# Products between matmul streams in the ffn stage and the last stage of a two-block transformer step on one core

## Chip, core and metric

One Trainium2 chip, one of its cores. The metric is the device time of one execution in microseconds.

## What is computed

Two transformer blocks over 256 tokens of 1024 features, fp32. Cut to what matters here:

```python
def conv_ffn(h, w_up, conv_w, conv_b, w_down, rows, cols):
    z = (h @ w_up).reshape(b, rows, cols, 2 * D_FF)
    z = lax.conv_general_dilated(z, conv_w[:, :, None, :], ...)
    z = z.reshape(b, l, 2 * D_FF) + conv_b
    return (jax.nn.silu(z[..., :D_FF]) * z[..., D_FF:]) @ w_down
...
        x = x + mx[:, :, 5] * conv_ffn(h2, ffn_up[layer], ...)   # first block
...
        h2 = rms_norm(x, norm2_g[l])                             # second block
        f = jnp.square(jax.nn.relu(jnp.einsum('bsd,df->bsf', h2, w_mlp1[l])))
        x = x + jnp.einsum('bsf,fd->bsd', f, w_mlp2[l])
```

The first block's ffn has 2 x 2816 inner features (22 chunks of `ffn_up`, 11 of `ffn_down`), the second block's has 4096 (16 chunks of `w_mlp1`, 16 of `w_mlp2`).

## The kernel before

**Tiles.** Activations lie with features on the partitions, as 8 tiles of 128 x 256 tokens. Weights come in chunks of 128 x 2048 through four `raw` buffers (DMA from the sync engine, line 413). ScalarE rounds a chunk to its high part `whi` (line 491), GpSimd (lines 467, 473) or VectorE (line 872) computes the low part `wlo = raw - whi`; there are three buffers of each. VectorE has the low parts of every `w_mlp2` chunk and of `w_mlp1` from chunk 3 on. Activations are split in the same way (H2h and H2l, H4h and H4l, AH and AL, FH and FL).

**Products.** `mm3` (lines 1456 to 1458) is three matmuls of 256 moving columns into one bank of PSUM: high by high, high by low, low by high. `pair` (line 1575) runs one chunk of `ffn_up` or `w_mlp1`: 8 tiles k, two outputs j, three matmuls, 48 in all; its `midway` callback is run ahead of tile n = 5. `contract` (line 1762) runs one chunk of `ffn_down` or `w_mlp2`, again 48 matmuls. Both name the chunk's weights through `weights`, which waits for the high and the low part.

**Small products.** In fp32, so each is two passes on the engine: the profile counts x2.
- `square_columns` (line 1723): a squared tile is the stationary side, a column of ones the moving side, one output column. It sums squares for a norm.
- `rows` (line 1460): a column of RC broadcast to 128 x 128 is stationary, the identity moves (128 columns). It spreads a scale over the partitions.
- `settle` (line 1756): eight products of 128 moving columns. Nobody reads their output.

**Order.** Each engine has one hand-written program, kept together by semaphores. In the ffn stage (line 1784) TensorE runs `ffn_up` 0, settle into banks 6 and 7, `ffn_up` 1 to 4 and then `ffn_up` and `ffn_down` in turn. In the last stage (line 1931) it runs `w_mlp1` 0, with `finish_norm` ahead of its tile 5 (eight column products that end the sum of squares of the last norm), then the two row products, settle into bank 3, `w_mlp1` 1, `w_mlp1` 2, `w_mlp2` 0, `w_mlp1` 3, `w_mlp2` 1 and so on.

**The scale of the last norm.** Columns (`col_x`), ScalarE's root (line 509), VectorE's reciprocal (line 884, `rstd_x`), the row products (`row_x`), ScalarE's copy to RR (line 851, `rr_done`), and VectorE's relu of `w_mlp1` 0, which multiplies by RR (line 1413). VectorE's program in this stage, per i: low parts up to the chunk two places ahead (`low`, line 1407), relu (1413), square (1419), low part of the activation (1423), and from i = 2 the low parts up to two places behind `w_mlp2` i - 2 (line 1426). ScalarE's runs alongside: high parts of weights and, behind each square, FH (line 861):

```python
        for i in range(18):
            if i < 16:
                low(turn["w_mlp1", i] + 2)
                if i == 0:
                    e.wait_ge(s["rr_done"], 3)
...
            if i >= 2:
                low(turn["w_mlp2", i - 2] + 2)
```

Of the kernel before, what the change touches and what calls it, by code (L numbers as in the profile page):

```python
# [14 lines left out]
P = 128  # L15
T = 256
D = 1024
KT = D // P
NH = 4
# [155 lines left out]
def build(nc, io):  # L175
# [6 lines left out]
    start = 16512  # L182
# [1251 lines left out]
    def tensor(e):  # L1434
# [137 lines left out]
                    m = e.matmul(b[:, hd * P:(hd + 1) * P], KM[:, hd, t * P:(t + 1) * P], q, start=True, stop=True)  # L1572
                m.then_inc(s["lev"], 1)

        def pair(name, i, xh, xl, ks=range(KT), ready=None, apart=False, midway=None):
            h, l = weights(name, i)
            bs = [group(name, i), group(name, i, 1)] if apart else [group(name, i)] * 2
            todo = [(n, k, j) for j in range(2) for n, k in enumerate(ks)] if apart else [
                (n, k, j) for n, k in enumerate(ks) for j in range(2)]
            for n, k, j in todo:  # L1580
                if midway and (n, j) == (5, 0):
                    midway()
                if ready and j == 0:
                    ready(k)
                m = mm3(bs[j][:, j * T:(j + 1) * T], h, l, (j * KT + k) * P, xh[:, k, :], xl[:, k, :],
                        n == 0 and (j == 0 or apart), n == len(ks) - 1)
                if n == len(ks) - 1 and (j or apart):
                    m.then_inc(s["gemm"], 1)
# [134 lines left out]
        def square_columns(b, sq, f, n):  # L1723
            for k in range(f, f + n):
                for t in range(2):
                    m = e.matmul(b[:, t:t + 1], sq[:, k, t * P:(t + 1) * P], ones[:, 0:1], start=k + t == 0,  # L1726
                                 stop=k == KT - 1, skip_group_check=True)
            return m
# [24 lines left out]
            e.wait_ge(s["h2_hi"], k + 1)  # L1753
            e.wait_ge(s["h2_lo"], k + 1)

        def settle(banks, w, x):
            for t, b in enumerate(banks):
                for k in range(NH):
                    e.matmul(b[:, k * P:(k + 1) * P], w[:, k, t * P:(t + 1) * P], x[:, k, t * P:(t + 1) * P],
                             start=True, stop=True)  # L1760

        def contract(name, j, xh, xl, slots, hi_sem, lo_sem, per, last):
            h, l = weights(name, j)
            ends_ = last == 2 * j + 1
# [18 lines left out]
            e.wait_ge(s[free[0]], free[1])  # L1783
        for i in range(24):
            if i == 1:
                settle((bank[6], bank[7]), TMP1, SQ1)
            if i < 22:
                pair("ffn_up", i, H2h, H2l, ready=h2_ready if i == 0 else None)
            if i >= 5 and i % 2:
                contract("ffn_down", (i - 5) // 2, AH, AL, NA, "a_hi", "a_lo", 1, 21)  # L1790
# [131 lines left out]

        def finish_norm():
            e.wait_ge(s["sq3_sum"], 2)
            square_columns(bs, SQ3, 0, 2)
            for j in range(2):
                e.wait_ge(s["sq3"], 4 + j)
                m = square_columns(bs, SQ3, 6 + j, 1)
            m.then_inc(s["col_x"], 1)

        for i in range(18):
            if i < 16:
                pair("w_mlp1", i, H4h, H4l, ready=h4_ready if i == 0 else None,
                     midway=finish_norm if i == 0 else None)
                if i == 0:
                    b = misc("rows3")
                    e.wait_ge(s["rstd_x"], 2)
                    rows(b, [wide(0), wide(1)], "row_x")
                    settle((bank[3], bank[3]), SQ3[:, 0:4, :], SQ3[:, 4:8, :])
            if i == 2:  # L1940
                for free in acc2_free:
                    e.wait_ge(s[free[0]], free[1])
            if i >= 2:
                contract("w_mlp2", i - 2, FH, FL, NF, "f_hi", "f_lo", 2, 31)
# [125 lines left out]
```

## Time and profile before

| | |
|---|---|
| median of 3 runs | 725.08 us (724.97, 725.08, 731.91) |
| profiled execution | 724.98 us |
| its span, first to last instruction | 723.0 us |
| mean granted clock of TensorE | 0.995 |
| TensorE busy | 710.7 us (98%) |
| VectorE, ScalarE, GpSimd busy | 483.5, 358.3, 389.1 us |
| HBM read, written | 143.88 MB, 1.05 MB |

PE is TensorE, DVE VectorE, ACT ScalarE, POOL GpSimd, SP the sync engine. The profile shows one execution. A matmul's own duration includes its way through the pipeline, so matmuls overlap: what TensorE gives to each is the distance of the starts, and a chunk's time is the distance between its first start and the next one's. L12 is line 12 of the kernel. Where a line of the timeline has a releaser in brackets, the engine was idle before it for that long.

### The profile page before, as it was taken

The numbers are of one execution on the slowest core, as the hardware profiler recorded it, in microseconds if no ns is written. First come the engines' busy times: TensorE is split into PE (matmuls) and PEld (weight loads), VectorE is DVE, ScalarE is ACT, GpSimd is POOL, SyncE is SP. The second block draws the span as 40 slices with busy tenths as digits, with TensorE's granted clock in tenths as the row PEclk, the third lists the DMA queues.
The fourth block names the chain that finished last, engine by engine and source line by source line (L and its number), as shares of the span: only waits on it lengthen the run. The fifth ranks groups of instructions, "written<-read, shape, count | busy, mean of one in ns | idle before, by whom it ended". The sixth has DMA issues, their size and how long they took to land.

```text
span 723.0 us, 14266 instructions
## 1 busy us (share of the span) xinstructions
PE 710.7 (98%) x5892; PEld 688.6 (95%) x5892; DVE 483.5 (67%) x906; ACT 358.3 (50%) x459; POOL 389.1 (54%) x219
## 2 busy tenths in 40 slices
PE   6899999999999999999999999999999999999998
PEld 3798889999999999999999999999999999999998
DVE  3886898469616459977777774657465666566563
ACT  6679235245434565455555456445754334334331
POOL 0767553547557948897888888765895000000000
PEclk9999999999999999999999999999999999999999
DMA  8995878336634637565655554433445564565611
GB/s 358 420 414 181 349 286 317 154 117 234 233 117 133 217 118 276 179 224 188 217 179 179 202 204 175 141 134 135 164 137 209 192 207 172 205 202 172 210 59 59
DMA packets 21234, 145.84 MB, mean 202 GB/s; under 512 B 2482, under 2 KB 3250, under 8 KB 3891
## 3 DMA queue, kind: packets, MB, share of 16 engines
q1 hardware_dynamic: 21024, 144.87, 55.0%
q8 instruction: 47, 0.77, 0.4%
q14 instruction: 17, 0.13, 0.0%
q10 hardware_dynamic: 146, 0.07, 0.0%
HBM read 143.88 MB, written 1.05 MB: 200 GB/s over the span
## 4 chain that ended last, share of the span: by engine, by line
PE 97%; DVE 1%; ACT 1%; issue 0%; DMA 0%; ACTq 0%; DVEq 0%
PE bank L1456 25%; PE bank L1458 25%; PE bank L1457 25%; PE bank L1475 5%; PE CP L1458 2%; PE CP L1456 2%; PE CP L1457 2%; PE bank L1572 2%; PE bank L1500 1%; PE bank L1533 1%; PE bank L1515 1%; PE CP L1489 1%; PE bank L1482 0%; PE bank L1684 0%; PE bank L1611 0%; PE bank L1726 0%
## 5 line engine op out<-in xcount | busy, mean ns | idle before, releaser
L473 POOL TENSOR_TENSOR wlo<-raw,whi 128x512 fp32r<-128x512 f32 (+1 forms) x185 | 353.3, 1941 | 136.8 <-ACT whi L491 136.7
L491 ACT ACTIVATE whi<-raw 128x2048 fp32r<-128x2048 f32 x100 | 191.3, 1913 | 46.2 <-DMA raw<-in_w_in 25.8
L1213 DVE SCALAR_TENSOR_TENSOR Y<-bank,vec,Y 128x189 f32<-128x189 f32 (+2 forms) x352 | 123.0, 423 | 35.2 <-ACT Y L746 35.2
L1456 PE MATMUL bank<-H2h,whi 128*128 128x256 f32 x352 | 97.7, 278 | 0.0
L1457 PE MATMUL bank<-H2l,whi 128*128 128x256 f32 x352 | 97.2, 276 | 0.0
L1458 PE MATMUL bank<-H2h,wlo 128*128 128x256 f32 x352 | 97.2, 276 | 0.0
L1456 PE MATMUL bank<-H1h,whi 128*128 128x256 f32 (+1 forms) x288 | 89.8, 312 | 2.3 <-ACT H1h L557 2.0
L1458 PE MATMUL bank<-H1h,wlo 128*128 128x256 f32 (+1 forms) x288 | 88.2, 306 | 0.0
L872 DVE TENSOR_TENSOR wlo<-raw,whi 128x2048 fp32r<-128x2048 f32 x29 | 66.7, 2300 | 32.2 <-ACT whi L491 32.2
L1457 PE MATMUL bank<-H1l,whi 128*128 128x256 f32 (+1 forms) x288 | 88.2, 306 | 0.0
L1456 PE MATMUL bank<-H4h,whi 128*128 128x256 f32 x256 | 70.9, 277 | 0.0
L1457 PE MATMUL bank<-H4l,whi 128*128 128x256 f32 x256 | 70.7, 276 | 0.0
L1458 PE MATMUL bank<-H4h,wlo 128*128 128x256 f32 x256 | 70.7, 276 | 0.0
L1456 PEld LDWEIGHTS bank<-H2h,whi 128*128 128x128 f32 x352 | 66.2, 188 | 0.1
L1457 PEld LDWEIGHTS bank<-H2l,whi 128*128 128x128 f32 x352 | 66.2, 188 | 0.1
L1458 PEld LDWEIGHTS bank<-H2h,wlo 128*128 128x128 f32 x352 | 66.2, 188 | 0.0
L1456 PEld LDWEIGHTS bank<-H1h,whi 128*128 128x128 f32 x288 | 54.9, 191 | 6.4 <-issue 3.3
L1458 PEld LDWEIGHTS bank<-H1h,wlo 128*128 128x128 f32 x288 | 54.9, 191 | 2.9
L1457 PEld LDWEIGHTS bank<-H1l,whi 128*128 128x128 f32 x288 | 54.9, 191 | 2.9
L467 POOL TENSOR_TENSOR wlo<-raw,whi 128x512 fp32r<-128x512 f32 x28 | 35.3, 1288 | 27.8 <-ACT whi L494 27.8
L1458 PEld LDWEIGHTS bank<-H4h,wlo 128*128 128x128 f32 x256 | 48.1, 188 | 0.0
L1456 PEld LDWEIGHTS bank<-H4h,whi 128*128 128x128 f32 x256 | 48.1, 188 | 0.0
(337 smaller groups left out, 1920.9 us busy)
## 6 DMA issues: line engine op xcount, KB each, us to landing
raw<-in_w_mlp SPq DMA_DIRECT2D x32, 1024.0 KB, 4.9
raw<-in_w_in SPq DMA_DIRECT2D x30, 1024.0 KB, 5.2
raw<-in_ffn_up SPq DMA_DIRECT2D x22, 1024.0 KB, 4.9
raw<-in_ada_hi SPq DMA_DIRECT2D x16, 1024.0 KB, 5.4
raw<-in_ffn_down SPq DMA_DIRECT2D x11, 1024.0 KB, 4.9
raw<-in_w_out SPq DMA_DIRECT2D x8, 1024.0 KB, 4.9
ada_s<-in_ada_s SPq DMA_DIRECT2D x4, 1024.0 KB, 18.0
ada_p<-in_ada_p SPq DMA_DIRECT2D x2, 1024.0 KB, 10.2
```

The source lines that it names most:

```text
L467: e.tensor_tensor(part(l, kp, 1), part(r, kp, 1), part(h, kp, 1).bitcast(F32), ALU.subtract).then_inc(s["lo_pool"], 1)
L473: m = e.tensor_tensor(l[:, a:a + step], r[:, a:a + step], h[:, a:a + step].bitcast(F32), ALU.subtract)
L491: e.activation(whi[q % NHI][:, :], raw[n % NRAW][:, :], ACT.Copy).then_inc(s["w_hi"], 1)
L872: e.tensor_tensor(l[:, :], r[:, :], h[:, :].bitcast(F32), ALU.subtract).then_inc(s["lo_dve"], 1)
L1213: e.scalar_tensor_tensor(o[:, r0:r1, c0:c1], z[:, r0 + dr:r1 + dr, c0 + dc:c1 + dc], cw[:, f, tap:tap + 1], o[:, r0:r1, c0:c1], ALU.mult, ...
L1456: e.matmul(out, h[:, col:col + P], xh, start=first, stop=False, skip_group_check=True)
L1457: e.matmul(out, h[:, col:col + P], xl, start=False, stop=False, skip_group_check=True)
L1458: return e.matmul(out, l[:, col:col + P], xh, start=False, stop=last, skip_group_check=True)
L1475: m = e.matmul(out, x, w, start=k + t + n == 0, stop=(k, n) == (KT - 1, 2), skip_group_check=True)
L1489: e.matmul(CP[:, half], ones[0:1, 0:P], CROW[:, half], start=True, stop=True).then_inc(s["c_spread"], 1)
L1500: m = e.matmul(out, C2[:, k, :], r[:, :, k, :], start=k == 0, stop=k == KT - 1)
L1572: m = e.matmul(b[:, hd * P:(hd + 1) * P], KM[:, hd, t * P:(t + 1) * P], q, start=True, stop=True)
```

## The change

TensorE's program alone is edited. In the ffn stage, settle between chunks 0 and 1 becomes eight column products of SQ1 into bank 6, and one row product into bank 7 is put between chunks 1 and 2. In the last stage settle is gone, the columns of the norm stand ahead of tile 7 of chunk 0 instead of tile 5 (with all squares waited for at their head), and the row products stand ahead of tile 5 of chunk 1 instead of behind chunk 0. `settle` itself is removed. The outputs of the new products in the ffn stage are read by nobody.

```diff
--- before.py
+++ after.py
@@ -1572,13 +1572,13 @@
                     m = e.matmul(b[:, hd * P:(hd + 1) * P], KM[:, hd, t * P:(t + 1) * P], q, start=True, stop=True)
                 m.then_inc(s["lev"], 1)
 
-        def pair(name, i, xh, xl, ks=range(KT), ready=None, apart=False, midway=None):
+        def pair(name, i, xh, xl, ks=range(KT), ready=None, apart=False, midway=None, at=5):
             h, l = weights(name, i)
             bs = [group(name, i), group(name, i, 1)] if apart else [group(name, i)] * 2
             todo = [(n, k, j) for j in range(2) for n, k in enumerate(ks)] if apart else [
                 (n, k, j) for n, k in enumerate(ks) for j in range(2)]
             for n, k, j in todo:
-                if midway and (n, j) == (5, 0):
+                if midway and (n, j) == (at, 0):
                     midway()
                 if ready and j == 0:
                     ready(k)
@@ -1753,12 +1753,6 @@
             e.wait_ge(s["h2_hi"], k + 1)
             e.wait_ge(s["h2_lo"], k + 1)
 
-        def settle(banks, w, x):
-            for t, b in enumerate(banks):
-                for k in range(NH):
-                    e.matmul(b[:, k * P:(k + 1) * P], w[:, k, t * P:(t + 1) * P], x[:, k, t * P:(t + 1) * P],
-                             start=True, stop=True)
-
         def contract(name, j, xh, xl, slots, hi_sem, lo_sem, per, last):
             h, l = weights(name, j)
             ends_ = last == 2 * j + 1
@@ -1783,7 +1777,9 @@
             e.wait_ge(s[free[0]], free[1])
         for i in range(24):
             if i == 1:
-                settle((bank[6], bank[7]), TMP1, SQ1)
+                square_columns(bank[6], SQ1, 0, NH)
+            if i == 2:
+                rows(bank[7], [wide(0)], None)
             if i < 22:
                 pair("ffn_up", i, H2h, H2l, ready=h2_ready if i == 0 else None)
             if i >= 5 and i % 2:
@@ -1922,21 +1918,19 @@
 
         def finish_norm():
             e.wait_ge(s["sq3_sum"], 2)
+            e.wait_ge(s["sq3"], 5)
             square_columns(bs, SQ3, 0, 2)
-            for j in range(2):
-                e.wait_ge(s["sq3"], 4 + j)
-                m = square_columns(bs, SQ3, 6 + j, 1)
-            m.then_inc(s["col_x"], 1)
+            square_columns(bs, SQ3, 6, 2).then_inc(s["col_x"], 1)
+
+        def finish_rows():
+            b = misc("rows3")
+            e.wait_ge(s["rstd_x"], 2)
+            rows(b, [wide(0), wide(1)], "row_x")
 
         for i in range(18):
             if i < 16:
                 pair("w_mlp1", i, H4h, H4l, ready=h4_ready if i == 0 else None,
-                     midway=finish_norm if i == 0 else None)
-                if i == 0:
-                    b = misc("rows3")
-                    e.wait_ge(s["rstd_x"], 2)
-                    rows(b, [wide(0), wide(1)], "row_x")
-                    settle((bank[3], bank[3]), SQ3[:, 0:4, :], SQ3[:, 4:8, :])
+                     midway={0: finish_norm, 1: finish_rows}.get(i), at=5 if i else 7)
             if i == 2:
                 for free in acc2_free:
                     e.wait_ge(s[free[0]], free[1])
```

TensorE, end of `ffn_up` chunk 0 and start of chunk 1 (bank<-H2h,whi_54 is chunk 0, whi_55 chunk 1; the number behind a buffer tells its copies apart). Before:

```order
L1456 MATMUL bank<-H2h,whi_54 128x256
L1457 MATMUL bank<-H2l,whi_54 128x256
L1458 MATMUL bank<-H2h,wlo_57 128x256
L1759 MATMUL bank<-SQ_130,TMP_131 128x128 x8
L1456 MATMUL bank<-H2h,whi_55 128x256
L1457 MATMUL bank<-H2l,whi_55 128x256
L1458 MATMUL bank<-H2h,wlo_58 128x256
```

After:

```order
L1456 MATMUL bank<-H2h,whi_54 128x256
L1457 MATMUL bank<-H2l,whi_54 128x256
L1458 MATMUL bank<-H2h,wlo_57 128x256
L1726 MATMUL bank<-ones,SQ_130 128x1 x8
L1456 MATMUL bank<-H2h,whi_55 128x256
L1457 MATMUL bank<-H2l,whi_55 128x256
L1458 MATMUL bank<-H2h,wlo_58 128x256
```

Eight products of 128 moving columns have given way to eight of one column. In the new order there is one more, at the end of chunk 1, ahead of chunk 2 (whi_53):

```order
L1456 MATMUL bank<-H2h,whi_55 128x256
L1457 MATMUL bank<-H2l,whi_55 128x256
L1458 MATMUL bank<-H2h,wlo_58 128x256
L1462 MATMUL bank<-con,RC 128x128
L1456 MATMUL bank<-H2h,whi_53 128x256
L1457 MATMUL bank<-H2l,whi_53 128x256
L1458 MATMUL bank<-H2h,wlo_56 128x256
```

This single row product has no counterpart before.

TensorE, last stage, end of chunk 0 (whi_53) and start of chunk 1 (whi_54) before:

```order
L1456 MATMUL bank<-H4h,whi_53 128x256
L1457 MATMUL bank<-H4l,whi_53 128x256
L1458 MATMUL bank<-H4h,wlo_56 128x256
L1462 MATMUL bank<-con,RC 128x128 x2
L1759 MATMUL CP<-SQ_160 128x128 x8
L1456 MATMUL bank<-H4h,whi_54 128x256
L1457 MATMUL bank<-H4l,whi_54 128x256
L1458 MATMUL bank<-H4h,wlo_57 128x256
```

And in the new order, the last six matmuls of chunk 0 with the columns ahead of them, and the first of chunk 1:

```order
L1458 MATMUL bank<-H4h,wlo_56 128x256
L1726 MATMUL bank<-ones,SQ_160 128x1 x8
L1456 MATMUL bank<-H4h,whi_53 128x256
L1457 MATMUL bank<-H4l,whi_53 128x256
L1458 MATMUL bank<-H4h,wlo_56 128x256
L1456 MATMUL bank<-H4h,whi_53 128x256
L1457 MATMUL bank<-H4l,whi_53 128x256
L1458 MATMUL bank<-H4h,wlo_56 128x256
L1456 MATMUL bank<-H4h,whi_54 128x256
```

Settle is gone and the columns have moved from 18 matmuls ahead of the chunk's end to 6. The row products now stand inside chunk 1, behind its 30th matmul:

```order
L1457 MATMUL bank<-H4l,whi_54 128x256
L1458 MATMUL bank<-H4h,wlo_57 128x256
L1462 MATMUL bank<-con,RC 128x128 x2
L1456 MATMUL bank<-H4h,whi_54 128x256
L1457 MATMUL bank<-H4l,whi_54 128x256
L1458 MATMUL bank<-H4h,wlo_57 128x256
```

So they come 30 matmuls later than before, counted from the end of chunk 0.

## Rows read from the trace of the kernel before

**Rows 1.** The page's chain that ended last, by engine (shares of the span).
```profile
PE 97%; DVE 1%; ACT 1%; issue 0%; DMA 0%; ACTq 0%; DVEq 0%
```

**Rows 2.** Timeline of PE, ffn stage: start us, us, engine line operation out<-in xcount.
```profile
267.30 1.95 PE L1759 MATMUL bank<-SQ,TMP 128*128 128x128 f32 x16
...
269.00 0.37 PE L1456 MATMUL bank<-H2h,whi 128*128 128x256 f32 x1
...
274.54 0.28 PE L1456 MATMUL bank<-H2h,whi 128*128 128x256 f32 x1
```

**Rows 3.** Timeline of PE, last stage.
```profile
541.34 0.28 PE L1456 MATMUL bank<-H4h,whi 128*128 128x256 f32 x1
...
544.75 1.86 PE L1726 MATMUL bank<-ones,SQ 128*128 128x1 f32 x16
...
546.47 0.36 PE L1456 MATMUL bank<-H4h,whi 128*128 128x256 f32 x1
...
548.67 0.65 PE L1462 MATMUL bank<-con,RC 128*128 128x128 f32 x4
...
549.16 1.95 PE L1759 MATMUL CP<-SQ 128*128 128x128 f32 x16
...
550.86 0.37 PE L1456 MATMUL bank<-H4h,whi 128*128 128x256 f32 x1
...
556.40 0.28 PE L1456 MATMUL bank<-H4h,whi 128*128 128x256 f32 x1
...
572.72 0.28 PE L1456 MATMUL CP<-FH,whi 128*128 128x256 f32 x1
```

**Rows 4.** Timeline of PE, around a chunk of w_in_2.
```profile
465.00 0.36 PE L1456 MATMUL bank<-H3h,whi 128*128 128x256 f32 x1
...
470.74 0.95 PE L1823 MATMUL bank<-con,SQq 128*128 128x2 f32 x8
```

**Rows 5.** PE by line, 465.3 to 470.7: xcount | busy us, mean ns | idle.
```profile
L1458 PE MATMUL bank<-H3h,wlo 128*128 128x256 f32 x16 | 4.5, 281 | 0.0
```

**Rows 6.** Windows of PE: busy us (x instructions), granted clock, DMA share, GB/s.
```profile
258.50:262.00 3.50, 3.50 (x11) 0.52 0.82 272
...
446.00:453.00 7.00, 7.00 (x64) 1.00 0.41 150
```

**Rows 7.** PE by line, 38 to 50 us.
```profile
L1458 PE MATMUL bank<-H1h,wlo 128*128 128x256 f32 x34 | 9.6, 281 | 0.0
```

**Rows 8.** Timeline of PE, row products in the w_in stage.
```profile
52.72 0.61 PE L1462 MATMUL bank<-con,RC 128*128 128x128 f32 x4
...
53.08 0.37 PE L1456 MATMUL bank<-H1h,whi 128*128 128x256 f32 x1
```

**Rows 9.** PE by line, 53.5 to 58.5 us.
```profile
L1458 PE MATMUL bank<-H1h,wlo 128*128 128x256 f32 x15 | 4.1, 276 | 0.0
```

**Rows 10.** Timeline of DVE, last stage.
```profile
543.70 1.46 DVE L1399 SCALAR_TENSOR_TENSOR H4l<-XR,vec,H4h 128x256 fp32r<-128x256 f32 x1 [0.89 <-ACT H4h L845]
...
549.77 0.69 DVE L1413 SCALAR_TENSOR_TENSOR FR<-bank,RR 128x512 f32<-128x512 f32 x1 [1.28 <-ACT RR L851]
...
553.79 2.51 DVE L872 TENSOR_TENSOR wlo<-raw,whi 128x2048 fp32r<-128x2048 f32 x1 [0.81 <-ACT whi L491]
...
556.60 0.69 DVE L1413 SCALAR_TENSOR_TENSOR FR<-bank,RR 128x512 f32<-128x512 f32 x1 [0.30 <-PE bank L1458]
...
566.66 2.29 DVE L872 TENSOR_TENSOR wlo<-raw,whi 128x2048 fp32r<-128x2048 f32 x1 [1.12 <-ACT whi L491]
...
572.92 0.69 DVE L1413 SCALAR_TENSOR_TENSOR FR<-bank,RR 128x512 f32<-128x512 f32 x1 [1.19 <-PE bank L1458]
```

**Rows 11.** Timeline of POOL, last stage.
```profile
548.23 5.92 POOL L473 TENSOR_TENSOR wlo<-raw,whi 128x512 fp32r<-128x512 f32 x4 [1.94 <-ACT whi L491]
```

**Rows 12.** Timeline of PE, a wait in the middle of a stream.
```profile
31.94 0.36 PE L1456 MATMUL bank<-H1h,whi 128*128 128x256 f32 x1 [1.96 <-ACT H1h L557]
```

**Rows 13.** PE by line, 31.2 to 33 us.
```profile
L1457 PE MATMUL bank<-H1l,whi 128*128 128x256 f32 x3 | 0.8, 279 | 0.0
```

## The prediction

> **What bounds the kernel now.** I read the page's chain of work first. It shows TensorE on 97% of the span, and nearly all of that in the three lines 1456 to 1458, the three products (high by high, high by low, low by high) of `mm3` [rows 1]. Two stages hang on it here: the ffn stage (chunks of `ffn_up` and `ffn_down`, from 261 us) and the last stage (`w_mlp1` and `w_mlp2`, 541 to 720 us). So whatever TensorE is given or spared counts in full, as long as the weights and activations that it reads are ready. The profiled execution took 724.98 us for a span of 723.0 us; the other 1.98 us lies around the span and the change does not touch it. My sum is made against 724.98, 0.10 below the median of 725.08.
>
> Next the timeline of TensorE at both places. In the ffn stage the eight "settle" products (16 passes, since an fp32 product is issued as two) start at 267.30 and the next chunk at 269.00: 1.70 us [rows 2]. That chunk of 48 matmuls takes 5.54 us (269.00 to 274.54). In the last stage chunk 0 starts at 541.34, its 16 column passes at 544.75, its last 18 matmuls at 546.47, the row products at 548.67, settle at 549.16, chunk 1 at 550.86, chunk 2 at 556.40, and the second `w_mlp2` chunk at 572.72 [rows 3]. From 556.40 to 572.72 there are three chunks of 48 matmuls, 5.44 us each, with no gap.
>
> **Two paces.** The extra products have no reader, so I looked for what they might do to their neighbours. The same 48 matmuls take 5.74 us after a burst of column products (465.00 to 470.74) [rows 4] against 5.54 after settle. The grouped lines say the same per instruction: a mean of 281 ns between 465.3 and 470.7 [rows 5], and 276 ns where the stream is fast. The starts are 0.118 us apart in the slow pace and 0.1133 in the fast one (5.44 / 48). The granted clock is 1.00, so 2.4 GHz, in both (446 to 453 us, which holds slow and fast matmuls) [rows 6]. What a burst leaves behind: a first matmul that is followed late, 0.10 us in all (5.54 less 5.44), and one of the two paces, which then lasts until the next burst. Columns leave the slow pace when they come out of the fast one: at 465.00, and at 546.47, where 18 matmuls take 2.20 us. Products with 128 moving columns leave the fast pace whatever came before: matmuls at 281 ns from 38 to 50 us, two row products at 52.72, and 276 ns from 53.5 us on [rows 7 to 9]. Settle is such a burst.
>
> **The ffn stage, term by term.**
> - Eight column products in place of eight 128-column products: 16 passes for 16. Columns took 1.72 us for 16 passes (544.75 to 546.47) with a pause of 0.02 in them, settle 1.70: 0.0.
> - Chunk 1 then runs at the slow pace: 5.74 instead of 5.54, +0.20.
> - One row product before chunk 2, two passes. Two products (four passes) took 0.36 (52.72 to 53.08) [rows 8]; less two passes of 0.11 (1.70 / 16) this leaves 0.14.
> - Chunk 2 now follows a burst and pays 0.10.
> - Chunks 3 and on: fast, if one row product does what two did. No row shows one alone.
> Sum +0.44 us. Nothing hides it, because nothing waits for TensorE to get earlier there.
>
> A rule speaks for another price. The Trainium skill, "TensorE: Matmul & The Clock Gate", section Back-to-back issue gap, gives about 60 cycles as the gap of a matmul with 1 to 64 moving columns, which is 25 ns; 16 column passes would by that take 0.4 us as an estimate and the ffn stage would win 1.3. The trace disagrees: 1.72 us for 16 passes, 107 ns each. The section LDWEIGHTS (loading the stationary operand) of the same page of the Trainium skill gives columns / 1.2, 107 ns for 128, per weight load, whatever the moving side; with that the trace agrees.
>
> **The last stage, term by term.** In the new order, in the old trace's clock: 42 fast matmuls from 541.34 take 4.77 (0.1136 each: 3.41 for 30), to 546.11. Columns 1.72, to 547.83. The last 6 matmuls of chunk 0, slow with the entry: 2.20 less 12 x 0.118, 0.79, to 548.62. Then 30 matmuls of chunk 1 at the slow pace, 3.54, to 552.16. Row products 0.36 (549.16 less 548.67 gives 0.49 where TensorE also waited a little for the root), to 552.52. Then 18 matmuls at the fast pace with the entry, 5.54 less 30 x 0.1133, 2.14: chunk 1 ends at 554.66 instead of 556.40. TensorE is 1.74 us earlier, nearly all of it the 1.70 of settle.
>
> Is the input there? The columns at 546.11 need the last square; the old order asked for it in its last column products, shortly before 546.47, and lost 0.02 there, so it is there by about 546.2. The tile k=6, which TensorE now reaches at 541.34 + 36 x 0.1136 = 545.43, needs the low part that VectorE ends at 543.70 + 1.46 = 545.16 [rows 10]. Both just fit; I book 0, and at worst 0.2. Chunk 2's low weights end on GpSimd at 548.23 + 5.92 = 554.15, for a chunk that now starts at 554.66: 0.5 us left [rows 11].
>
> What the moved rows delay: the scale RR is copied from them, and VectorE's queue is in order: relu of chunk 0, its square and low part, the low weights of `w_mlp2` chunk 0, relu of chunk 1, and so on. In the old trace the rows start at 548.67 and this relu at 549.77; the new rows start at 552.16 and last 0.13 less, so relu starts at about 553.15. From there to the end of the low weights of `w_mlp2` 0 it was 6.53 us (549.77 to 553.79 + 2.51), in part beside GpSimd; I take 6.2 to 6.5: 559.35 to 559.65. TensorE wants them at 554.66 + 5.44 = 560.10: in time. Relu of chunk 1 started at 556.60, when the chunk was done; now it stands behind these low weights and starts at their end. From it to the end of the low weights of `w_mlp2` 1 (566.66 + 2.29 = 568.95) it was 12.35 us of VectorE and ScalarE in turn with no wait for TensorE. So these end at 571.7 to 572.0 [rows 10]. TensorE, 1.74 earlier, wants them at 572.72 - 1.74 = 570.98, and waits about 0.8 us. It starts this chunk at about 571.8 instead of 572.72. Of the 1.74 only 0.92 is kept. Behind that VectorE catches up: the old trace shows it 1.19 us idle ahead of the relu at 572.92, and the pattern repeats with every pair of chunks, so nothing further is lost.
>
> **Sum:** +0.44 - 0.92 = -0.48 us. 724.98 - 0.48 = 724.5 us.
>
> **Rivals.**
> 1. No stall: the chain on VectorE is shorter than I add up, or TensorE's need is later. The full 1.74 is kept: -1.30, 723.7. For it: only 0.7 to 1.0 us decides.
> 2. The ffn stage stays slow: one row product does not restore the pace. Against it: two do, and every 128-column burst looked at. For it: no row shows one, and the execution at 731.91 beside 724.97 shows that some 7 us can come and go in this very kernel. From chunk 2 on there are 20 chunks of `ffn_up` and 11 of `ffn_down`: 31 x 0.20 to 0.22 = 6.5. Gives 731.0, slower than before.
> 3. The last stage stays slow: the new wait in front of a `w_mlp2` chunk, with no burst behind it, could leave the slow pace to the end. Of waits in the middle of a stream one row speaks: after 1.96 us of idle at 31.94 the three high-by-low matmuls behind it have a mean of 279 ns, between 281 (slow) and 276 (fast), so it speaks for neither clearly [rows 12, 13]. From 571.8 to 719.6 there are 27 chunks: 27 x 0.21 = 5.7. Gives 730.2. If the rows fail too, some 0.6 more. Both 2 and 3: 736.7.
> 4. The clock: the granted clock fell to 0.52 of full in 258.5 to 262.0, after columns and a thin stretch [rows 6], and settle may be there to keep it up. Against it: 446 to 453 holds twice 16 column passes and keeps 1.00. If it fell once, 3.4 us at half would cost about 1.7: 726.2.
>
> **Chances.** Forecast 0.45; rival 1 0.12; rival 2 alone 0.14; rival 3 alone 0.15; both 0.08; rival 4 and small mishaps 0.06. The predicted time is the likeliest case's, 724.5 (its own range 723.4 to 725.6). The range goes from 723.3 to 731.6: it takes in rivals 1, 2 and 3 one at a time and leaves out both together. One per cent, about what a measurement of this kernel can tell from no change, is 7.25 us: a single slow stage stays below it, two do not. Faster by over 1%: 0.02. Within 1%: 0.87. Slower by over 1%: 0.11.
>
> **What would show it.** In the new timeline: columns of 1.70 us at 267.3 and chunk 1 at 5.74; a gap of about 0.14 before chunk 2, which takes 5.54, and 5.44 in every later chunk (5.65 if rival 2 holds). In the last stage: columns at about 546.5 (the ffn stage's 0.44 added), rows at 552.6, and a wait of some 0.8 us in front of the second `w_mlp2` chunk, with VectorE's low weights as its releaser. Means of 281 ns after it would be rival 3. A granted clock under 1.00 after 262 us would be rival 4. I am wrong in the mechanism if chunk 1 of the ffn stage is fast, or if chunk 2 is slow.

## The result, and the profile after

| | before | after |
|---|---|---|
| median | 725.08 us | 731.6 us |
| lowest, highest of 20 executions | 723.7, 732.7 | 729.3, 738.6 |
| profiled execution, its span | 724.98, 723.0 | 731.20, 729.3 |
| mean granted clock of TensorE | 0.995 | 0.999 |
| ratio after / before | | 1.0089, 95% interval 1.0061 to 1.0117 |

The changed kernel is 6.5 us slower, where I had forecast it 0.5 faster: inside the band of 1%, at the edge of the range (731.6), and 7.1 us from the 724.5 that I forecast. It is the time of rival 2 (731.0). One plain fact is needed to read the numbers below: executions of one and the same kernel fall on levels some 6 to 7 us apart (before: 14 of 20 at 723.7 to 725.8 and 6 at 731.4 to 732.7; after: 12 at 729.3 to 732.2 and 8 at 736.9 to 738.6), so beside each median I give how many lie on which level, while the ratios leave out what is over 1.5% above the fastest of its kernel (of before, a third level at 737 and up that later sets have).

The timeline of TensorE in the ffn stage of the kernel after, which answers to [rows 2]:

```profile
266.26 1.84 PE L1726 MATMUL bank<-ones,SQ 128*128 128x1 f32 x16
...
267.96 0.36 PE L1456 MATMUL bank<-H2h,whi 128*128 128x256 f32 x1
...
273.70 0.38 PE L1462 MATMUL bank<-con,RC 128*128 128x128 f32 x2
...
273.84 0.36 PE L1456 MATMUL bank<-H2h,whi 128*128 128x256 f32 x1
...
279.57 0.28 PE L1456 MATMUL bank<-H2h,whi 128*128 128x256 f32 x1
```

The column products take 1.70 us (266.26 to 267.96), the chunk behind them 5.74, the row product 0.14 (two passes), just as booked. (A pass is one of the two that an fp32 product is issued as, a burst a group of such products in the stream, and the pace is the distance of the starts of the large matmuls: 113.3 ns fast, 117.8 ns slow.) But the chunk behind the row product again takes 5.73 us (273.84 to 279.57), where a chunk at the fast pace with its entry takes 5.54. It never comes back. Grouped by line over the rest of the stage, 279.5 to 440 us (xcount, then busy us and mean ns), first after, then before:

```profile
L1458 PE MATMUL bank<-H2h,wlo 128*128 128x256 f32 x305 | 85.7, 281 | 0.0
```

```profile
L1458 PE MATMUL bank<-H2h,wlo 128*128 128x256 f32 x306 | 84.5, 276 | 0.0
```

Mean 281 against 276 ns over 305 matmuls of one line, the two numbers by which [rows 5] and [rows 9] told the paces apart. The clock is not it. Windows of TensorE after (busy us and instructions, granted clock, DMA share, GB/s), to be held against the 0.52 of [rows 6]:

```profile
258.50:262.00 3.50, 3.50 (x23) 1.00 0.79 293
268.00:449.00 181.00, 181.00 (x1538) 1.00 0.56 195
```

Both are at 1.00, 2.4 GHz. The 181 us from 268 are at full clock and TensorE is busy in all of them, which is why the page's first part cannot show the loss: 98% busy in both kernels.

The last stage of the kernel after, which answers to [rows 3]:

```profile
548.31 0.28 PE L1456 MATMUL bank<-H4h,whi 128*128 128x256 f32 x1
...
553.25 1.84 PE L1726 MATMUL bank<-ones,SQ 128*128 128x1 f32 x16
...
554.96 0.36 PE L1456 MATMUL bank<-H4h,whi 128*128 128x256 f32 x1
...
559.28 0.61 PE L1462 MATMUL bank<-con,RC 128*128 128x128 f32 x4
...
559.64 0.37 PE L1456 MATMUL bank<-H4h,whi 128*128 128x256 f32 x1
...
567.22 0.28 PE L1456 MATMUL CP<-FH,whi 128*128 128x256 f32 x1
...
572.78 0.36 PE L1456 MATMUL bank<-H4h,whi 128*128 128x256 f32 x1
...
578.91 0.36 PE L1456 MATMUL CP<-FH,whi 128*128 128x256 f32 x1 [0.23 <-issue]
```

Chunk 0 still runs slow (42 matmuls in 4.95 us), the rows at 559.28 bring back the fast pace, and then TensorE waits twice: the last matmul before 572.78 is followed after 0.24 us instead of 0.113, and the one before 578.91 after 0.51. VectorE in the same stretch says for what:

```profile
560.34 0.69 DVE L1413 SCALAR_TENSOR_TENSOR FR<-bank,RR 128x512 f32<-128x512 f32 x1 [4.75 <-ACT RR L851]
...
564.27 2.29 DVE L872 TENSOR_TENSOR wlo<-raw,whi 128x2048 fp32r<-128x2048 f32 x1 [1.12 <-ACT whi L491]
...
566.48 0.68 DVE L1413 SCALAR_TENSOR_TENSOR FR<-bank,RR 128x512 f32<-128x512 f32 x1
...
570.39 2.29 DVE L872 TENSOR_TENSOR wlo<-raw,whi 128x2048 fp32r<-128x2048 f32 x1 [1.11 <-ACT whi L491]
...
576.51 4.49 DVE L872 TENSOR_TENSOR wlo<-raw,whi 128x2048 fp32r<-128x2048 f32 x2 [1.11 <-ACT whi L491]
```

The low weights of `w_mlp1` 3 end at 570.39 + 2.29 = 572.68 and its chunk starts 0.10 later. The row of 576.51 holds two chunks' low weights; one of them takes 2.29, which puts the end of the first, `w_mlp2` 1, at 578.80, and its chunk starts 0.11 later. Between the two waits the mean is 281, and behind the second it is 276 to the end:

```profile
L1458 PE MATMUL bank<-H4h,wlo 128*128 128x256 f32 x12 | 3.4, 281 | 0.0
```

```profile
L1458 PE MATMUL bank<-H4h,wlo 128*128 128x256 f32 x163 | 45.0, 276 | 0.0
```

So the pace changed at waits too, with no burst near them, once in either direction here.

**Where the 6.3 us of span are.** After less before, read at the same places of the two timelines: -1.04 at the burst behind chunk 0 (266.26 less 267.30; the half clock of [rows 6] is absent in this execution); -0.70 at the start of chunk 2, so the new bursts and the slow chunk 1 cost 0.34; -0.41 at its end; then 30 chunks of 5.653 instead of 5.440 add 6.40, which makes +5.99 at the end of the stage. It is +6.13 at `w_out` of the second block, whose 4 chunks ran slow here as well and add 0.84: +6.97 at chunk 0 of the last stage; at `w_mlp2` 1 at +6.19 (578.91 less 572.72), so this stage gained 0.78; at the end +6.3.

### The profile page after: what moved, and what is told of

Read it like the earlier page. It is cut to its first block, busy times and chain, and to the rows that moved or that the text cites. A ratio compares the mean times of both kernels' runs of the same rounds, so it can differ in the third digit from the quotient of the medians.

```text
span 729.3 us, 14239 instructions
## 1 busy us (share of the span) xinstructions
PE 716.6 (98%) x5878; PEld 693.4 (95%) x5878; DVE 482.1 (66%) x906; ACT 358.2 (49%) x459; POOL 389.5 (53%) x219
## 4 chain that ended last, share of the span: by engine, by line
PE 97%; DVE 1%; ACT 1%; issue 0%; DMA 0%; ACTq 0%; DVEq 0%
PE bank L1456 25%; PE bank L1457 25%; PE bank L1458 25%; PE bank L1475 5%; PE CP L1456 2%; PE CP L1458 2%; PE CP L1457 2%; PE bank L1572 2%; PE bank L1500 1%; PE bank L1726 1%; PE bank L1515 1%; PE CP L1489 1%; PE bank L1482 0%; PE bank L1684 0%; PE bank L1611 0%
## 5 line engine op out<-in xcount | busy, mean ns | idle before, releaser
L1456 PE MATMUL bank<-H2h,whi 128*128 128x256 f32 x352 | 99.6, 283 | 0.0
L1457 PE MATMUL bank<-H2l,whi 128*128 128x256 f32 x352 | 98.9, 281 | 0.0
L1458 PE MATMUL bank<-H2h,wlo 128*128 128x256 f32 x352 | 98.9, 281 | 0.0
```

The costliest lines, as they stand in the source:

```text
L1456: e.matmul(out, h[:, col:col + P], xh, start=first, stop=False, skip_group_check=True)
L1457: e.matmul(out, h[:, col:col + P], xl, start=False, stop=False, skip_group_check=True)
L1458: return e.matmul(out, l[:, col:col + P], xh, start=False, stop=last, skip_group_check=True)
```

## The experiments

**Which half of the change costs it.** Three kernels: the change with a second row product in the ffn stage (r1), the last stage's edits alone (r2), the ffn stage's alone (r5: after with `settle`, `finish_norm` and the rows of the last stage as before).

```diff
             if i == 2:
-                rows(bank[7], [wide(0)], None)
+                rows(bank[7], [wide(0), wide(1)], None)
```

> The changed kernel with two row products (four passes) instead of one ahead of ffn_up chunk 2. Theory 'burst too short': one row product leaves the slow pace standing, two end it. Then chunk 2 takes 5.54 us, chunks 3 and on 5.44 instead of 5.65, and the whole is 6.3 us faster than the changed kernel, near 724.5 to 725. Rival 'columns': the eight column products put the engine into a pace that no row products end here; then chunks stay at 5.65 and the time near 731.5. Rival 'last stage': the loss is made there, in the waits behind the moved rows; then 731.5 as well, with fast chunks in the ffn stage.

> The ffn stage of the kernel before (settle), the last stage of the changed one. Theory 'burst too short': the loss lies in the ffn stage alone, so this is 0.5 to 1.3 us faster than the kernel before (724 us), with one or two waits of 0.1 to 0.8 us near the first w_mlp2 chunks. A pace drawn at random at those waits would put some executions near 730. Rival 'last stage': 731, slower by some 6 us, mostly.

> The ffn stage of the changed kernel (columns, then one row product), the last stage of the kernel before. Theory 'burst too short': the pace stays slow through 31 chunks, the time is 731 to 732 mostly. Rival 'last stage': 725.5 with fast ffn chunks.

| | median us | before beside it | ratio, 95% | levels |
|---|---|---|---|---|
| r1 | 729.4 | 725.6 | 1.001 (0.997 to 1.005) | 3 of 10 at 724.1 to 725.5, 7 at 729.1 to 730.5 |
| r2 | 724.3 | 725.6 | 0.997 (0.993 to 1.001) | 6 of 10 at 723.0 to 724.4, 3 at 729.4 to 730.1, 1 at 735.5 |
| r5 | 734.5 | 731.7 | 1.010 (1.001 to 1.020) | 2 of 4 at 731.5 to 731.8, 2 at 737.3 to 737.7 |

r1's timeline at the second burst, and the means behind it:

```profile
274.55 0.61 PE L1462 MATMUL bank<-con,RC 128*128 128x128 f32 x4
...
274.91 0.37 PE L1456 MATMUL bank<-H2h,whi 128*128 128x256 f32 x1
```

```profile
L1458 PE MATMUL bank<-H2h,wlo 128*128 128x256 f32 x306 | 84.5, 276 | 0.0
```

Four passes instead of two, 0.36 us instead of 0.14, and the whole stage is at 276 ns. That is the point on which the forecast rested. r5 has one row product and 281 ns over the same stretch, and none of its four executions is near 724. The ffn edit alone reproduces the loss, by the trace and the levels (four executions are too few for the ratio to carry it); the last stage's edit alone does not.

r2's profiled execution (730.14 us) shows the other mechanism. Its ffn stage is at 276 ns. The last stage:

```profile
566.10 0.36 PE L1456 MATMUL bank<-H4h,whi 128*128 128x256 f32 x1
...
572.22 0.36 PE L1456 MATMUL CP<-FH,whi 128*128 128x256 f32 x1 [0.23 <-issue]
```

```profile
L1458 PE MATMUL bank<-H4h,wlo 128*128 128x256 f32 x192 | 54.0, 281 | 0.0
```

These are the same two waits as after (0.24 and 0.51 us between starts). Fast ahead of the first, at 281 ns behind it, and here the second wait did not give the fast pace back: to the end the stage is slow, some 6 us, which is rival 3 in one execution. In r1 the same two waits (0.24 and 0.71) left the fast pace alone.

**Is it the number of passes?** One traced execution each (753.6, 768.9 and 757.8 us, long because of the many bursts), with a burst ahead of every `ffn_up` chunk from 1 to 21, r for row products, c for columns, then their number. r3 and r4 wrote them into the bank of the chunk behind, r7 into another; `settle` in the ffn stage is gone, the rest is as before. r3 had r8 c8 r1 r1 r2 c8 r2 c8 r3 c8 r1 r4 c4 r1 r2 c2 r2 c1 r1 r8 c8, r4 r8 c8 c8 c8 r8 c4 c4 r8 c2 c2 r8 c1 c1 c1 r8 c16 c16 r8 c8 c8 c8, and r7:

```diff
+        BURSTS = [('c', 8), ('r', 1), ('c', 8), ('r', 2), ('c', 8), ('r', 3), ('c', 8), ('r', 1),
+                  ('c', 8), ('r', 2), ('c', 8), ('r', 4), ('c', 8), ('r', 1), ('r', 1), ('c', 8),
+                  ('r', 2), ('r', 1), ('c', 8), ('r', 8), ('c', 1)]
...
             if i == 1:
-                settle((bank[6], bank[7]), TMP1, SQ1)
+            if 1 <= i <= 21:
+                burst(i)
```

> The kernel before without settle in the ffn stage, and with a burst of extra products ahead of each ffn_up chunk 1 to 21 instead (rows r or columns c, and how many products): r8 c8 r1 r1 r2 c8 r2 c8 r3 c8 r1 r4 c4 r1 r2 c2 r2 c1 r1 r8 c8. No output of theirs is read. Theory 'burst too short': the 48 matmuls behind each r2, r3, r4 and r8 have 276 ns and 5.54 us, those behind c8 281 ns and 5.74; those behind r1 keep the pace that stood before. Rival: the pace behind a burst does not depend on its kind or length, and r1 is followed by the fast pace about as often as r2.

> The same with the bursts r8 c8 c8 c8 r8 c4 c4 r8 c2 c2 r8 c1 c1 c1 r8 c16 c16 r8 c8 c8 c8. Theory: any column burst that comes out of the fast pace leaves the slow one; out of the slow pace the outcome was mixed in the two traces (at 471.55 in the trace of before fast, at 477.68 in the one after slow), so I expect some of each; all r8 are followed by the fast pace. Rival: short column bursts (c1, c2) leave the fast pace standing.

> As the sweep of rows, but each burst writes another PSUM bank than the matmuls behind it (in the first sweeps it was the same one, in the kernel it is another). Bursts: c8 r1 c8 r2 c8 r3 c8 r1 c8 r2 c8 r4 c8 r1 r1 c8 r2 r1 c8 r8 c1 (the last in its own bank). Theory 'length and bank': r2, r3, r4 and r8 are all followed by the fast pace, r1 out of the slow pace by the slow one. Rival 'drawn at random': rows are followed by either pace here too, as in the first sweeps.

In the same bank (r3, r4) the rule of "two or more" failed: from the slow pace two passes gave the fast one in 2 of 5 bursts, four in 2 of 3, sixteen in 3 of 5. With another bank, as in the kernel, the outcomes in this stage are clear. Of r7 two bursts out of the slow pace, with the chunk behind each:

```profile
332.39 0.38 PE L1795 MATMUL bank<-con,RC 128*128 128x128 f32 x2
...
351.36 0.61 PE L1795 MATMUL bank<-con,RC 128*128 128x128 f32 x4
```

```profile
L1458 PE MATMUL bank<-H2h,wlo 128*128 128x256 f32 x13 | 3.7, 281 | 0.0
```

```profile
L1458 PE MATMUL bank<-H2h,wlo 128*128 128x256 f32 x14 | 3.9, 276 | 0.0
```

The two rows of means are of the chunks behind 332.39 (two passes: 281, slow) and 351.36 (four passes: 276, fast). Out of the slow pace, one row product restored it in 0 of 4, two in 3 of 3, four and eight in 1 of 1 each; three (six passes) did not, in the only try. Counted over the matmul starts of all 16 traces of this case (bursts of 128 moving columns, without those of r3 and r4 in the bank of the chunk behind, from 130 us on), out of the slow pace: two passes 0 of 7, four 15 of 15, six 0 of 1, eight 17 of 17, sixteen 33 of 34.

Ahead of 130 us the rule is weaker. The two row products near 52 us, the burst of [rows 8], also write another bank. They came out of the slow pace in 11 of the 16 traces and left it slow in four (r3, r5, r10, r14), in r3 with no wait about them (its timeline, and its matmuls from 53.5 to 58.5 us):

```profile
52.36 0.60 PE L1462 MATMUL bank<-con,RC 128*128 128x128 f32 x4
...
52.72 0.36 PE L1456 MATMUL bank<-H1h,whi 128*128 128x256 f32 x1
```

```profile
L1458 PE MATMUL bank<-H1h,wlo 128*128 128x256 f32 x15 | 4.2, 281 | 0.0
```

So it is no threshold: two passes out of the slow pace never restored it in another bank (0 of 7), four did in 22 of 26.

Columns. r4's eight column products (sixteen passes) all came out of the slow pace and left it slow, 6 of 6; of fewer columns a single one once gave the fast pace. Over the 16 traces sixteen column passes that came out of the fast pace ended slow in 24 of 30; the six exceptions are all in the last stage. There all nine such bursts had a short wait in them (0.02 to 0.08 us), as one in r7 had that ended slow; the 20 with no wait in them ended slow each time. Fewer passes act otherwise: eight passes with two moving columns, in the stage of [rows 4], turned slow into fast in 22 of 25 and fast into slow in 23 of 23. One of them stands in the trace of before, at the end of the slow chunk of [rows 4] (the timeline, and the matmuls from 471.9 to 476.8 us):

```profile
470.74 0.95 PE L1823 MATMUL bank<-con,SQq 128*128 128x2 f32 x8
...
471.55 0.36 PE L1456 MATMUL bank<-H3h,whi 128*128 128x256 f32 x1
```

```profile
L1458 PE MATMUL bank<-H3h,wlo 128*128 128x256 f32 x15 | 4.1, 276 | 0.0
```

So 128 moving columns are not what it takes to end the slow pace. r4's clock fell to half (0.50) at 413.5 to 420.3 us, behind two bursts of 32 column passes (401.4 and 410.6); the pace was slow ahead of it and fast (113.3) when the clock came back, with no burst in between, so a change of the clock can go with one of the pace too.

**Does the kernel need settle?** r6 puts two row products in the place of the ffn stage's settle and drops the other one. r9 does this with a second burst of two row products in each stage (ahead of `ffn_up` chunk 3 and of `w_mlp1` chunk 2), to give a stage that comes out slow another try. r11 is r6 again, for a second trace.

```diff
             if i == 1:
-                settle((bank[6], bank[7]), TMP1, SQ1)
+                rows(bank[7], [wide(0), wide(1)], None)
...
                     rows(b, [wide(0), wide(1)], "row_x")
-                    settle((bank[3], bank[3]), SQ3[:, 0:4, :], SQ3[:, 4:8, :])
```

> The kernel before with settle gone from both stages: two row products stand in its place in the ffn stage, and in the last stage the row products that are there anyway remain where they were, at the end of chunk 0. Theory: two row products set the fast pace as settle did, at 0.36 us instead of 1.70, and in the last stage settle was not needed: 725.0 - 1.34 - 1.70 = 722.0, with no wait behind the row products. Rival 'settle is needed': the pace after four passes is slow in one stage or both, 728 or more.

> Another trace of the run without settle. If the execution is on one of its upper levels (727.5 or 735), the trace shows which stage is slow: theory, matmuls at 281 ns from a burst to the end of its stage.

> The run without settle (two row products in its place) with one more burst of two row products in each stage: ahead of ffn_up chunk 3, and ahead of w_mlp1 chunk 2. Each burst costs 0.36 + 0.10 us. Theory: the levels of the time, some 7 us apart, are the pace that a burst leaves; a burst of two row products ends the slow pace where the first one failed, so the upper levels (727, 735) become rarer, with the lowest at 721.4. Rival 'drawn before the burst': the levels come from elsewhere (clock, DMA) and stay as frequent as without it.

| | median us | before beside it | ratio, 95% | levels |
|---|---|---|---|---|
| r6 | 727.8 | 731.7 | 0.996 (0.991 to 1.001) | 3 of 10 at 720.5 to 721.9, 6 at 727.4 to 729.6, 1 at 735.1 |
| r9 | 729.1 | 724.5 | 0.999 (0.993 to 1.004) | 4 of 12 at 722.2 to 722.6, 4 at 728.4 to 729.7, 4 at 734.7 to 735.8 |

The price of the two settles is as read: r6's fastest execution (720.46) lies 3.2 us under that of before beside it (723.62), against 1.34 + 1.70 = 3.04 worked out. The levels stay. r11 (728.46 us) is r6 with its ffn stage slow: the row products at 267.06 came out of a fast chunk and left it slow. r9's second burst did not make the upper levels rarer: its third level is as full as its second. Its trace shows why: in the ffn stage the first burst (266.26) came out of the fast pace and left it slow, and the second (278.01) brought it back, but in the last stage the extra rows at 552.93 met the fast pace and left it slow. A second try is not free, because it also acts on a stream that is fast already.

**Is before's upper level the same thing?** r8 is the kernel before once more, at 733.13 us.

> The kernel before, unchanged, for another trace of it. If its execution falls on the upper of its two levels (near 731), one stage of its trace shows matmuls at 281 ns over about 30 chunks, or some 6 us lie elsewhere; if on the lower, it repeats the trace there is.

```profile
267.63 1.95 PE L1759 MATMUL bank<-SQ,TMP 128*128 128x128 f32 x16
...
269.33 0.36 PE L1456 MATMUL bank<-H2h,whi 128*128 128x256 f32 x1
```

```profile
L1458 PE MATMUL bank<-H2h,wlo 128*128 128x256 f32 x307 | 86.3, 281 | 0.0
```

In this execution it is. The sixteen passes of settle at 267.63 came out of the slow pace and did not end it, the one case in 34, and the ffn stage is at 281 ns to its end. So the 731.91 beside 724.97 that I quoted under rival 2 may well have been an ffn stage at the slow pace (it was not traced), and of after's 20 executions none lies on the level near 724.

**Can both waits and the slow stage be had away?** r10 is r1 with the rows of the norm back at the end of chunk 0, so that no low weights are late; r12 is r1 again for a second trace; r13 is r1 with these rows ahead of tile 2 of chunk 1; r14 is after with them there and its one row product kept.

```diff
-                     midway={0: finish_norm, 1: finish_rows}.get(i), at=5 if i else 7)
+                     midway={0: finish_norm, 1: finish_rows}.get(i), at=2 if i else 7)
```

> The changed kernel with two row products ahead of ffn_up chunk 2 and with the last stage's row products back at the end of chunk 0 (columns still ahead of tile 7). Theory: the wait in front of the first w_mlp2 chunks is gone, and with it the pace drawn there; against the run with two rows alone the lowest level is 0.9 lower (723.3) and the level near 729.5 is rarer. Rival: the moved rows cost nothing, and the levels are as frequent as there (3 of 10 low).

> Another trace of the changed kernel with two row products. If on its upper level (729.5): theory, the ffn stage is fast and the last stage slow from the wait near w_mlp2 chunk 0 on; rival, the ffn stage is slow as in the changed kernel.

> The changed kernel with two row products ahead of ffn_up chunk 2, and the last stage's row products ahead of tile 2 of chunk 1 instead of tile 5, 2 us earlier. Theory: columns bring the stream to the slow pace and two row products from there to the fast one, every time, if nothing waits at the burst; at tile 2 the reciprocal is ready, and the scale is early enough that no wait for weights follows. Then ffn and last stage are fast in nearly every execution: 10 of 12 or more within 1 us of 723.4, median near 723.5. Rival 'drawn elsewhere': half the executions stay near 729.5, as with the rows at tile 5 or at the end of chunk 0.

> The changed kernel with only the last stage's row products moved to tile 2 of chunk 1. Theory: one row product leaves the ffn stage slow each time (+6.5), the last stage is fast each time: one level at 730, and the one at 737 is gone. Rival: two levels, 730.5 and 737, as in the changed kernel.

| | median us | before beside it | ratio, 95% | levels |
|---|---|---|---|---|
| r10 | 726.8 | 724.5 | 0.999 (0.995 to 1.004) | 6 of 12 at 723.0 to 724.6, 6 at 729.0 to 730.5 |
| r13 | 728.9 | 730.9 | 0.999 (0.995 to 1.002) | 3 of 12 at 722.6 to 723.6, 9 at 728.5 to 730.0 |
| r14 | 735.8 | 730.9 | 1.007 (1.002 to 1.012) | 4 of 10 at 729.3 to 730.1, 6 at 735.7 to 737.0 |

r12's execution took 723.7 us, with both waits and the last stage fast in its trace; r10's traced one 723.8, without a wait. In r10, r12 and r13 the ffn stage is at 276 ns, with r1 four traces of four with two row products; after, r5 and r14 are three of three at 281 with one. r13 and r14 differ in this one product and in nothing else, and their levels lie 7 us apart (middle of the lower ones 722.8 and 730.0, of the upper ones 729.0 and 736.1), of which 31 x 0.21 is 6.6. That settles the first half: in this kernel one row product ahead of chunk 2 leaves the ffn stage slow and two leave it fast.

The second half fell. I had held the two waits to be what draws the last stage's pace, and expected 10 of 12 executions of r13 on the low level; it was 3. Its trace (728.95 us):

```profile
545.44 1.92 PE L1726 MATMUL bank<-ones,SQ 128*128 128x1 f32 x16
...
549.37 0.60 PE L1462 MATMUL bank<-con,RC 128*128 128x128 f32 x4
```

```profile
L1458 PE MATMUL bank<-H4h,wlo 128*128 128x256 f32 x5 | 1.4, 276 | 0.0
```

```profile
L1458 PE MATMUL bank<-H4h,wlo 128*128 128x256 f32 x219 | 61.5, 281 | 0.0
```

No chunk waits for weights here. The columns took 1.78 us, with a wait of some 0.08 in them for the last square, and came out fast (276). Then the four row passes at 549.37, the very burst that restores the pace out of slow, turned it slow to the end. r14 shows the same at 556.28, and so do r9 at 266.26 and 552.93 and r11 at 267.06. Over the whole of the 16 traces, four row passes straight out of the fast pace left it slow in 8 of 8 (one of them in the bank of the chunk behind); where TensorE had waited ahead of them (last distance 155 ns or more) it stayed fast in 5 of 5. With settle right behind such row products, as in before's last stage, the stream ended slow in 2 of 2 (r3 at 570.60, r4 at 586.04, both after a wait of 0.03 us). So four row passes don't set a pace, they mostly turn the one that they meet into the other: out of the slow pace 22 of 26 ended fast. This is read from the traces of runs made for other questions. Bursts of 16 or 32 passes out of the fast pace, with 116 or 117 ns ahead of them, stayed fast in 144 of 144; all but two of these (the settle of before and of r2) are other products, in the stages ahead of the ffn stage.

Ahead of the five bursts named, the last interval was 115 ns and not 116 or 117. That looks like a cause and does not hold as one. Every burst of row products straight out of the fast pace begins 115 ns behind the last matmul, 12 of 12, and one of them (r7, two passes at 425.98) stayed fast; so did two bursts of sixteen other passes in r3 with 115 ns ahead. No run tried four row passes against four passes of another kind out of the fast pace.

This reading also says which way r13's last stage goes, though no run tests it by itself: columns that come out slow hand the rows a slow stream, which the rows turn fast (r1, r2, after); columns that come out fast, as they did in 6 of the 10 cases with a wait in them, hand them a fast one, which they turn slow (r13, r14).

**A version that beats both?** r2 and r6 have the lowest ratios (0.997 and 0.996), and r6 the lowest level (720.5), but no interval in the tables lies below 1. With every execution counted, r6 would be at 0.994 and r13 at 0.995, with upper ends at about 1.000 and 0.999; since the shares of before's levels differ from set to set, I claim none.

## Why the prediction was wrong, and where it was right

By its own steps:

- "Chunks 3 and on: fast, if one row product does what two did": this is the step that failed. It does not, in 7 tries of 7. It costs 31 x 0.21 = 6.6 us, of which the forecast had none: nearly the whole of the 6.7 between 724.5 and the profiled execution's 731.2. That rival 2's 731.0 comes so close is in part luck: -1.04 ahead of chunk 1 (mostly the half clock), +0.14 behind the ffn stage and +0.84 in `w_out`, none of them in my sum, cancel. The reason I gave for it was that "every 128-column burst looked at" restored the pace, but every such burst had four passes or more; the trace of before held no case of two, and I gave it 0.14. I also read that trace too narrowly: at 470.74 eight passes with two moving columns end the slow pace, so the width that I held to matter was not what did it.
- "Products with 128 moving columns leave the fast pace whatever came before": too strong as well. Four row passes straight out of the fast pace ended slow in 8 of 8, settle itself once in r8, and the very burst of [rows 8] left the slow pace standing in 4 of 11 traces.
- "Chunk 2 pays 0.10": it paid 0.30, entry and slow pace; by the same cause.
- Columns for settle, 0.0: right (1.70 for 1.70). Chunk 1 at the slow pace, 5.74: right (5.735). One row product 0.14: right (0.140).
- The last stage, -0.92: measured -0.78 by places of the timelines. Settle's 1.70 is gone as booked. The wait is there and VectorE's low weights end it, at 578.80 where my chain, moved by the 6.97 that TensorE entered the stage later, said 578.7 to 579.0. I had one wait of 0.8; up to this place it is 0.81, but of other parts: two waits, 0.13 + 0.39 (0.24 less 0.113 and 0.51 less 0.118), and between them a chunk at the slow pace with its entry, 0.21 + 0.08. The front of the document gives VectorE the low weights of `w_mlp1` from chunk 3 on, and I did not ask when those end: the waiting begins one chunk earlier than I said. Of the 0.14 that is missing, 0.11 is the time from the end of these low weights to the start of the chunk, which I had put at nothing. Chunk 0, which came in at the slow pace (4.95 for 4.77), moved the rows by 0.15, but VectorE's chain behind them was as much shorter (18.46 from the relu to the end of the low weights, where I had 18.55 to 18.85).
- "The columns need the last square; just fit, 0 or at worst 0.2": 0 after, where chunk 0 ran slow and so came later; 0.08 in r13, where it ran fast. Small in time, but such a wait in the columns goes with their coming out fast (6 of 10 against 0 of 20), and with that the row products behind them turn the stage slow (r13, r14). r12 had the same 0.08 and its columns came out slow, so the wait does not decide it alone. That was seen and not tried by itself.
- Rival 3 is real and stands beside rival 2, not against it: r2's trace shows it, and 8 of after's 20 executions at 736.9 to 738.6 lie close to the 736.7 that I gave for both; r14's trace at 736.0 has both stages slow. After itself was not traced on that level, so for it this is argued and not shown.
- Rival 4 (the clock): no. The granted clock from 258.5 to 262 us was 0.52 to 0.59 in before, r8, r3 and r7 and 1.00 in the other twelve traces, after among them. It lies ahead of the edit, where the program is the same in all, and from 262 to 265 us, still ahead of settle, the clock was back at 0.95 or more. After had 1.00 from 268 to 449.

The Trainium skill, "TensorE: Matmul & The Clock Gate", Back-to-back issue gap, gives 262 cycles as the gap of a warm matmul of 256 columns taken alone, 109 ns as an estimate. The traces differ: they have two values, 113.3 and 117.8 ns, both at granted clock 1.00. The columns of the ffn stage took 106 ns a pass (1.70 / 16). That agrees with the same page of the Trainium skill, section LDWEIGHTS (loading the stationary operand), columns / 1.2 or 107 ns for 128, as an estimate.

**What stays open.** What in TensorE the two paces are; why six passes failed once where four and eight did not; why the two row products near 52 us failed in 4 of 11 traces; what decides the pace behind a wait, and so why a kernel's last stage comes out anew in each execution. The share of executions on before's lowest level was 14 of 20, 10 of 19, 4 of 13, 12 of 23 and 6 of 23 in five sets, with no edit at all, and in the last four sets 1, 3, 4 and 7 of its executions lay at 737.1 to 738.8, where after's upper level lies.

## What to carry to other kernels

A burst of small fp32 products in a stream of dense matmuls costs more than its own time: it also changes or keeps the pace of everything up to the next burst or wait, 4% here, with busy share and clock unchanged. What it does depends on the pace that it meets as well as on its own length: the two row products that mend a slow stream spoil a fast one. Read it from the distance of two chunk starts, on both sides of every burst, and treat "half as many products do the same" as an unknown of the size of the whole stage (here 6.6 us against 0.22 saved). Where executions fall on levels, compare the levels and how many lie on each, trace one of each, and don't put a draw down to the edit.

## What the runs showed of the hardware that I had not expected

- Back-to-back fp32r matmuls of 128 x 256 start 113.3 or 117.8 ns apart at the same granted clock of 1.00 and keep to one of the two over 160 us and more.
- Out of the slow pace, in another bank, two fp32 passes of 128 moving columns left it slow 7 times of 7 and four made it fast 22 times of 26 (15 of 15 behind 130 us), though the two bursts differ by 0.22 us.
- Some bursts turn the pace into the other one whichever they meet: four row passes (slow to fast 22 of 26, fast to slow 8 of 8 with no wait ahead), and eight passes with two moving columns (slow to fast 22 of 25, fast to slow 23 of 23).
- The first distance behind a burst of 2 to 16 passes with 128 moving columns, out of the slow pace, already tells the pace to come (16 traces, from 130 us on): it was 205 to 210 ns in 70 of the 72 ahead of the fast pace (201 in two that had a wait inside the burst), and 200 or 201 in all 17 ahead of the slow one.
- A wait of 0.13 us in a stream changed the pace of what followed (after, r2) or not (r1, r12).
